# Up projection of a split-precision MLP: transposes one slot apart, squares right behind them, a weight combination ahead of an addition

## The reference

```python
h = rmsnorm(x, mix_norm[0])
b_gate, c_gate, v = jnp.split(h @ w_in, 3, axis=-1)      # 2048 -> 3 x 2048
u = c_gate * v
y = causal_depthwise_conv(u, conv_w)                      # width 3
x = x + (b_gate * y) @ w_out                              # 2048 -> 2048
h = rmsnorm(x, mlp_norm[0])
a = jax.nn.relu(h @ w1)                                   # 2048 -> 8192
x = x + (a * a) @ w2                                      # 8192 -> 2048
```

## Time and profile before

| | |
|---|---|
| median of 3 runs | 2013.15 us |
| lowest and highest | 2010.29 and 2013.25 us |
| the profiled execution | 2010.38 us |
| its span, first to last instruction | 2008.7 us |
| mean granted clock of TensorE | 0.995 |
| busy: TensorE, VectorE, ScalarE | 98%, 74%, 43% |
| up projection (about 704 to 1405 us of the span) | TensorE waits in the even v |
| down projection (about 1405 to 2004 us) | TensorE without a gap |

### The profile page before, as it was taken

How to read it: one execution, slowest core, us unless ns; L and a number is a source line. 1 busy time by engine, 2 the same in 40 slices (tenths; PEclk the granted TensorE clock), 3 DMA queues, 4 the chain that set the end, 5 groups by cost and what they waited for, 6 DMA issues and landing times. The chain is left out here.

```text
span 2008.7 us, 22945 instructions
## 1 busy us (share of the span) xinstructions
PE 1967.4 (98%) x8778; PEld 1625.4 (81%) x8778; DVE 1481.7 (74%) x1368; ACT 854.8 (43%) x1002; POOL 75.3 (4%) x146
## 2 busy tenths in 40 slices
PE   8999999999999999999999999999999999999999
PEld 7888888888888877778787787877888888888887
DVE  6345353363453589899898999989889879978878
ACT  6222222222234465655656566565444333433332
POOL 0000000000000100101101010010000000000000
PEclk9999999999999999999999999999999999999999
DMA  5323222232223545757677576779889788887783
GB/s 189 109 101 105 84 101 96 96 105 84 105 101 109 194 148 224 291 190 309 232 295 276 197 289 249 292 276 371 323 339 381 302 332 312 306 331 304 274 330 129
DMA packets 98317, 445.92 MB, mean 222 GB/s; under 512 B 10800, under 2 KB 10800, under 8 KB 73776
## 3 DMA queue, kind: packets, MB, share of 16 engines
q1 hardware_dynamic: 78944, 375.42, 49.7%
q0 software_dynamic: 19136, 69.21, 8.5%
q10 hardware_dynamic: 144, 0.04, 0.0%
HBM read 371.24 MB, written 73.40 MB: 221 GB/s over the span
## 5 line engine op out<-in xcount | busy, mean ns | idle before, releaser
L1082 PE MATMUL pair<-ring,act 128*128 128x512 f32 x5376 | 1237.1, 391 | 1.4 <-issue 0.8
L1082 PEld LDWEIGHTS pair<-ring,act 128*128 128x128 f32 x5376 | 1011.6, 189 | 212.9 <-issue 2.1
L454 ACT ACTIVATE ring<-raw 128x1024 fp32r<-128x1024 f32 x448 | 469.2, 1059 | 625.5 <-PE pair L1082 402.7
L797 DVE TENSOR_TENSOR ring<-raw,ring 128x1024 fp32r<-128x1024 f32 x448 | 539.9, 1220 | 133.1 <-ACT ring L454 131.2
L599 DVE TENSOR_TENSOR w_lo<-w_raw,w_hi 128x512 fp32r<-128x512 f32 x256 | 175.4, 692 | 349.0 <-ACT w_hi L377 343.7
L377 ACT ACTIVATE w_hi<-w_raw 128x512 fp32r<-128x512 f32 x256 | 161.5, 631 | 474.7 <-PE pair L987 471.7
L987 PE MATMUL pair<-h_hi,w_lo 128*128 128x512 f32 x764 | 297.8, 390 | 0.0
L987 PE MATMUL pair<-h_hi,w_hi 128*128 128x512 f32 x764 | 297.2, 389 | 0.0
L987 PE MATMUL pair<-h_lo,w_hi 128*128 128x512 f32 x764 | 297.2, 389 | 0.0
L792 DVE TENSOR_TENSOR raw<-raw 128x2048 f32<-128x2048 f32 x128 | 292.7, 2287 | 5.6
L987 PEld LDWEIGHTS pair<-h_hi,w_lo 128*128 128x128 f32 x764 | 143.4, 188 | 30.4 <-issue 0.8
(11 more groups left out here) (89 smaller groups left out, 747.2 us busy)
## 6 DMA issues: line engine op xcount, KB each, us to landing
raw<-in_mlp SPq DMA_DIRECT2D x128, 1024.0 KB, 7.7
act<-spill SPq DMA_DIRECT2D x224, 512.0 KB, 6.3
w_raw<-in_weights SPq DMA_DIRECT2D x63, 1024.0 KB, 4.9
spill<-stage POOLq DMA_DIRECT2D x112, 512.0 KB, 8.5
act<-act_kept SPq DMA_DIRECT2D x84, 512.0 KB, 6.8
act_kept<-act POOLq DMA_DIRECT2D x12, 512.0 KB, 6.5
mixed<-turned POOLq DMA_DIRECT2D x16, 256.0 KB, 2.9
x<-mixed SPq DMA_DIRECT2D x8, 512.0 KB, 11.1
```

Of the source, the lines that this page charges most:

```text
L454: nc.scalar.activation(ring[g % RING][:, 0], raw[:, r, 2 * (s % 2):2 * (s % 2) + 2, :], ACT.Copy).then_inc(hi_ready, 1)
L797: nc.vector.tensor_tensor(ring[g % RING][:, 1], raw[:, RAW_OF[s // 2], 2 * (s % 2):2 * (s % 2) + 2, :], ring[g % RING][:, 0].bitcast(F32), ...
L1082: mm = nc.tensor.matmul(bank, stationary, moving, start=(opens and k == 0 and n == 0), stop=(closes and k == NT - 1 and n == 2))
```

## The change

Three orders of issue change; nothing that is computed does, and the number of instructions is the same.

1. TensorE: the four groups of transposes stood ahead of slots 0, 2, 3 and 4 of the even v, and now stand ahead of slots 0, 1, 2 and 4.
2. ScalarE: the squares stood in slots 3, 5, 6 and 7, behind the rectification of the same slot. They are now in slots 3, 4, 5 and 7, ahead of it.
3. VectorE: addition 12 of slot 3 stood ahead of T2 and is now behind it.

With these the splits and forms of the quadrants move by up to two slots, three of them from one slot of the odd v, or the last of the even v, to the next.

```diff
-SPLIT_AT = {(0, 4): 0, (0, 6): 1, (0, 8): 2, (0, 10): 3, (0, 12): 4, (1, 0): 5, (1, 3): 6}
-FORM_AT = {(0, 9): (0, 1), (0, 12): (2,), (1, 1): (3,)}
+SPLIT_AT = {(0, 6): 0, (0, 7): 1, (0, 9): 2, (0, 11): 3, (0, 13): 4, (1, 1): 5, (1, 3): 6}
+FORM_AT = {(0, 10): (0, 1), (0, 13): (2,), (1, 2): (3,)}
...
                     if 2 <= v <= UP and v % 2 == 0:
+                        if s in (3, 4, 5, 7):
+                            square_quad(q - 1, {3: 0, 4: 1, 5: 2, 7: 3}[s])
                         if s in (2, 3, 4):
                             rectify(q - 1, s - 1)
-                        if s in (3, 5, 6, 7):
-                            square_quad(q - 1, {3: 0, 5: 1, 6: 2, 7: 3}[s])
...
-                        if s == 3:
-                            add_up(q - 1, 12)
...
                     if s == 3:
                         form_weights(v, T2)
+                        if 0 < v <= UP and v % 2 == 0:
+                            add_up(q - 1, 12)
...
-                        if 2 <= v <= UP and v % 2 == 0 and s in (0, 2, 3, 4):
-                            turn_quad(v // 2 - 1, {0: 0, 2: 1, 3: 2, 4: 3}[s])
+                        if 2 <= v <= UP and v % 2 == 0 and s in (0, 1, 2, 4):
+                            turn_quad(v // 2 - 1, {0: 0, 1: 1, 2: 2, 4: 3}[s])
```

## The result

The changed kernel takes 2001.31 us (median of 5 runs, 2000.15 to 2001.88); the kernel before took 2012.77 us beside it (2010.24 to 2013.25). The ratio is 0.9946, 95% interval 0.9932 to 0.9961: 0.54% faster. Forecast were 2000.5 us and a range of 1995.5 to 2007.5. The profiled execution has a span of 1999.6 us, 9.1 us less than before.

The account below looks back on a forecast made before the run. TensorE, busy 98%, bounds the kernel; its waits and slow clock cost some 34 us. Savings 2.96 + 1.5 + 6.4 - 0.7 = 10.2 us from 2010.4 give 2000.2, plus a little: 2000.5 us, range 1995.5 to 2007.5.

Parts of the forecast that it names:

- the hold at slot 12: TensorE in the odd v: slot 12 may wait for the addition reading its bank, 0 to 0.3 us seven times, net nothing.
- Part 1: Quadrant splits and forms moved: one more VectorE operation behind its last wait for TensorE, everything up to T1 1.14 us later.
- part 3: VectorE, T2 ahead of addition 12: the passed addition (1.13 us) pays almost exactly for the operation moved with the quadrant work.
- The clock: TensorE at 1.2 GHz after long waits: five of eight transitions slowed, 1.60 us each, 8.0 us in all, expected to go.
- no slow slots: TensorE transitions: longest stretch without slot matmuls falls to 2.15 + 0.8 us, so no granted clock of 0.50 expected.
- Rival A: TensorE transitions: the clock still falls, 5 to 13 us back, time 2005 to 2013; chance 0.14 together with no effect.
- Rival C: VectorE: two more operations behind its last wait, 16 us, transpose waits of 4.4 us, slow clock back, 2014 to 2024; chance 0.04.
- Part 4: ScalarE's second square right behind slot 4's copy: third transposes at 10.43 instead of 13.42, about 0.2 us won, 1.0 us waiting.

## Why the prediction was right, and where it was not

**The terms.** Slot 4 of a middle transition was put at T0 + 17.64 and is at 17.50; the waits were put at 2.15 and 1.0 us and are 1.8 and 0.9. T1 was put at T0 - 0.85 and is at -1.02. The difference of 0.17 us is the one cost that no row had shown: the hold at slot 12, bounded at 0 to 0.3 us and called neutral because it delays T0 and shortens the next wait by as much. The weight load row shows it (it stood idle 0.28 us). The other half of the 0.35 us by which the first wait was put too long is a due time: the second group was due at 3.77 (5.59 - 1.82) and not at 3.6. Neither moves the end of the chain through VectorE and ScalarE, so neither costs time: the spacing fell from 83.27 to 83.07 us, by 0.20 where 0.25 was forecast. The last transition lost 0.6 us where 0.7 was forecast.

**Part 1** was right, and both directions of it were tried: one operation behind the point costs 7.9 us by the sum, and taken away it gave 8.7, 8.0 of it in the transitions. The passing of addition 12 in part 3 was said to pay for it; taking part 3 away costs 7.8 us.

**The clock** carries 8 of the 9.1 us between the profiled executions. The ten filling matmuls show that this term is separate. But one step of the argument for its going was wrong: that a stretch like that after 2.37 us of waiting is safe, since the one example had kept its clock. By the runs the same wait slows some transitions and not others there, and what decides between them stays open. Transitions slowed, by the wait before the third group (two numbers joined by "and": the waits before the second and the third):

| kernel | waits, us | slowed |
|---|---|---|
| before | 3.28 to 3.76; 2.37 | 5 of 7; 0 of 1 |
| before, quadrant work later | 0.3 and 3.74 to 3.76; 2.81 | 7 of 7; 1 of 1 |
| before, T2 first | 2.97; 2.52 to 2.56; 1.61 | 1 of 1; 2 of 6; 0 of 1 |
| before, split later | 2.81; 2.34 to 2.38 | 1 of 1; 2 of 7 |
| changed, without part 3 | 1.8 and 1.87 | 1 of 8 |
| changed; with old tables; two operations later | 0.8 to 1.8 and 0.9 | 0 of 24 |
| changed, quadrant work early | 1.8 and 0.9; a lone 1.82 in the odd v | 0 of 8; 1 of 1 |
| before, filled | 1.03 to 1.50; 0.1 | 0 of 7; 0 of 1 |

The longest wait of the changed kernel, 1.8 us, is shorter than those that slowed two in seven, and no fall followed it in its eight transitions. But the lone 1.82 us shows that this length is not safe in itself, so "no slow slots" held in part by luck, and not because of the example that I gave. Rival A, short waits that bring the clock down, is real at 1.8 and 1.9 us, once in eight; whether the second wait is needed for it is not shown. That is the case for which the Trainium skill was cited ahead (TensorE: Matmul & The Clock Gate, section "A second HAM failure mode: psum-queue depth-cycling"): this row agrees with it in kind, the changed kernel does not show it.

**Rival C** had the right price (2.3 us for each of seven transitions, 2017.8 us) and the wrong place. In the changed kernel more lag of VectorE does not reach the transposes: the addition before slot 12 of the odd v takes it first, and there it brought no slow clock.

**What the prediction did not look for.** Part 4 of its sum said that moving the groups one slot earlier eats 2.77 of the 3.0 us that the early squares win, and went on. Run back, this is 22 us (2001.3 to 1979.2). The numbers for it were in the prediction: the second square lets the third group start at T0 + 10.43, and in its old place the group would be due at about 6.34 + 0.8 + 2.77 = 9.9, so some 0.5 us of waiting in place of 2.15 + 1.0.

## What to carry to other kernels

When a consumer in a hand-laid order is waiting, bringing its producer forward and moving the consumer forward are two changes; walk each alone, since the second can give back what the first wins. Look on each engine for the last point at which it still waits for the engine that bounds the kernel: work moved across that point was paid in full on every round here, work put into a gap where the engine waits for a copy anyway cost nothing. A TensorE wait has a second price here, about 1.6 us of slow clock in some of the rounds: in 5 of 7 at 3.28 us and more, in 2 of 7 at some 2.35 us, and in single cases at 1.8 us. Shorter waits, also when they come from splitting a long one, win most of that back.

## What the runs showed of the hardware

- The granted clock fell to 0.50, so to 1.2 GHz, after waits of 2.34 to 2.38 us in two of seven transitions and not in the other five, with the same code and the same waits within 0.04 us; one example can't tell a safe length. Each of these falls cost about 1.6 us.
- It fell to 0.50 as well after a lone wait of 1.82 us in an otherwise dense stretch (a kernel whose eight transitions, with waits of 1.8 and 0.9 us, kept it full).
- Ten matmuls of 128x512 with no use, put into a 3.3 us wait, took 9 us off the kernel's time and delayed nothing: 2003.09 us against 2012.08 in the same comparison.
- Five staging buffers with a median of 8.5 us to landing carry seven splits spread over 14 slots without a wait (so do 12, where the median was 9.2 us), but not within 10 slots (8.8 us): VectorE then waited 21.0 us for them in seven pairs.
